# Two level products joined, small products moved, and a last norm by token blocks in a two-layer hybrid decoder kernel

## What is computed

```python
for l in range(2):
    h = rmsnorm(x, norm1)
    qa, ka, va, hb, gate_b, gate_c, qc, fc, ic, og, zg = split_in(h @ w_in)   # 1024 -> 6400 columns
    ya = dilated window attention of (rope(qa), rope(ka), va)                 # 3 groups, 2 heads of 64 each
    yb = gate_b * conv(gate_c * hb)
    log_f, kgate = forget gate of fc
    # gated linear recurrence, per head and chunk:
    #   att[t, s] = sum_c q[t, c] * k[s, c] * exp(b[t, c] - b[s, c])   for s <= t,  b = cumsum(log_f)
    oc, s_fin = hgrn2(qc, log_f, kgate, ic)
    mix = g0 * (ya @ w_pa) + g1 * (yb @ w_pb) + g2 * (yc @ w_pc)
    x = x + mix @ w_o
    x = x + square(relu(rmsnorm(x, norm2) @ w_up)) @ w_down
return rmsnorm(x, norm_f), new caches and states
```

## Time and profile before

| | us |
|---|---|
| median of 3 runs | 827.78 (827.65 to 829.39) |
| the profiled execution's own time | 829.25 |
| its span, first to last instruction | 827.5 |
| PE busy | 816.1 (99% of the span) |
| DVE busy | 570.0 (69%) |
| ACT busy | 436.8 (53%) |
| POOL busy | 264.2 (32%) |
| mean granted PE clock | 0.995 |

### The profile page before, as it was taken

One profiled execution on the slowest core, in us unless ns is written; L12 is line 12 of the kernel. 1 busy time (PEld: TensorE's weight loads), 2 busy tenths in 40 slices (PEclk: granted clock), 3 DMA queues, 4 the chain that ended last, 5 costly groups with the idle time before them and its releaser, 6 DMA issues.

```text
span 827.5 us, 18120 instructions
## 1 busy us (share of the span) xinstructions
PE 816.1 (99%) x7016; PEld 801.4 (97%) x7016; DVE 570.0 (69%) x768; ACT 436.8 (53%) x621; POOL 264.2 (32%) x230
## 2 busy tenths in 40 slices
PE   9999999999999999999999999999999999999995
PEld 8999999999999999999999999999999999999995
DVE  7778787676877666554576688957787776645553
ACT  6553376645557665434353634774555666643442
POOL 4585282036710000121147825801565000001220
PEclk9999999999999999999999999999999999999999
DMA  9896859767657778776659968887665876776751
GB/s 314 235 319 256 301 162 324 237 227 269 218 179 253 240 241 306 248 262 226 205 164 247 312 234 278 241 259 256 232 237 179 260 247 221 260 280 234 250 203 52
DMA packets 171035, 200.00 MB, mean 242 GB/s; under 512 B 19680, under 2 KB 168496, under 8 KB 169648
## 3 DMA queue, kind: packets, MB, share of 16 engines
q1 hardware_dynamic: 169584, 197.02, 72.4%
q10 hardware_dynamic: 1392, 2.15, 0.7%
HBM read 191.25 MB, written 51.90 MB: 294 GB/s over the span
## 4 chain that ended last, share of the span: by engine, by line
PE 95%; DVE 3%; DMA 0%; ACT 0%; issue 0%; DVEq 0%; ACTq 0%
PE main L644 28%; PE main L645 28%; PE main L646 27%; PE small L694 2%; PE small L660 1%; PE small L646 1%; PE small L645 1%; PE small L644 1%; DVE w_lo L1189 1%; PE small L705 1%; DVE h_lo L1205 0%; DMA raw<-in_w_in 0%; PE small L798 0%; PE small L853 0%; PE small L722 0%; PE main L615 0%
## 5 line engine op out<-in xcount | busy, mean ns | idle before, releaser
L954 ACT ACTIVATE w_hi<-raw 128x1024 fp32r<-128x1024 f32 (+1 forms) x256 | 266.2, 1041 | 247.9 <-PE main L646 186.9
L1189 DVE TENSOR_TENSOR w_lo<-raw,w_hi 128x1024 fp32r<-128x1024 f32 (+1 forms) x256 | 337.3, 1318 | 64.6 <-ACT w_hi L954 60.6
L644 PE MATMUL main<-h_hi,w_hi 128*128 128x264 f32 x1264 | 365.6, 289 | 0.9 <-DVE w_lo L1189 0.8
L645 PE MATMUL main<-h_lo,w_hi 128*128 128x264 f32 x1264 | 358.8, 284 | 0.0
L646 PE MATMUL main<-h_hi,w_lo 128*128 128x264 f32 x1264 | 358.6, 284 | 0.0
L644 PEld LDWEIGHTS main<-h_hi,w_hi 128*128 128x128 f32 x1264 | 238.7, 189 | 5.9 <-DVE w_lo L1189 1.7
L645 PEld LDWEIGHTS main<-h_lo,w_hi 128*128 128x128 f32 x1264 | 239.0, 189 | 0.2
L646 PEld LDWEIGHTS main<-h_hi,w_lo 128*128 128x128 f32 x1264 | 237.6, 188 | 0.0
L644 PE MATMUL main<-a_hi,w_hi 128*128 128x264 f32 x512 | 145.3, 284 | 0.0
L645 PE MATMUL main<-a_lo,w_hi 128*128 128x264 f32 x512 | 145.0, 283 | 0.0
L646 PE MATMUL main<-a_hi,w_lo 128*128 128x264 f32 x512 | 145.0, 283 | 0.0
(11 more groups left out here) (222 smaller groups left out, 1030.0 us busy)
## 6 DMA issues: line engine op xcount, KB each, us to landing
raw<-in_w_in SPq DMA_DIRECT2D x48, 1024.0 KB, 5.8
raw<-in_w_up SPq DMA_DIRECT2D x32, 1024.0 KB, 5.3
raw<-in_w_down SPq DMA_DIRECT2D x32, 1024.0 KB, 5.2
out_kvs<-in_cache SPq DMA_DIRECT2D x48, 512.0 KB
out_kvs<-in_cache SPq DMA_DIRECT2D x32, 496.0 KB
raw<-in_w_o SPq DMA_DIRECT2D x8, 1024.0 KB, 5.3
raw<-in_w_br SPq DMA_DIRECT2D x8, 768.0 KB, 5.1
gates<-q_scratch SPq DMA_DIRECT2D x4, 768.0 KB, 7.2
```

Of the source, the lines that this page charges most:

```text
L644: pe.matmul(out[:, 0:TOK], wh, rh, start=start and k == 0, stop=False)
L645: pe.matmul(out[:, 0:TOK], wh, rl, start=False, stop=False)
L954: act.activation(w_hi[:, slot(l, u), 0:k, :], raw_of(u, k), ACT.Copy).then_inc(w_hi_ready, 1)
L1189: dve.tensor_tensor(w_lo[:, slot(l, u), 0:k, :], raw_of(u, k), w_hi[:, slot(l, u), 0:k, :].bitcast(F32), ALU.subtract).then_inc(w_lo_ready, 1)
```

## The change

It has six parts. (1) Levels 0 and 1 of the recurrence become one group, `first_levels`, behind unit 8: 8 products with 192 moving columns, the queries of the diagonal (copied by ACT into `q_first` behind output 5) beside the scaled odd queries of level 1, against the same keys. Their turns are 3 to 6, one for each pair of heads and half; level 2 keeps 7 and 8. DVE masks them all behind output 9 (`mask_first_levels`): four copies of 128 x 256 and four of 127 x 128. (2) "state" goes from unit 18 to 19, "sample kv T" from 20 to 21, "kv T 1" and "kv T 2" from 26 to 28, "attend" from 33 to 35, each ahead of the small product that was there. ACT's copies and DVE's copy move along. (3) In the last norm the squares become the stationary operand and one column of ones the moving one, so that tokens lie on partitions: three columns of sums. Root and reciprocal work on 128 x 3; three products of the broadcast reciprocal with the identity bring it back onto all partitions in PSUM. (4) In the head, `split_lo` of unit 6 goes ahead of `bounds`, that of unit 7 ahead of the forget gate. (5) Units 6 and 7 of layer 0 also take their low products last. (6) ACT issues the first weight piece ahead of the gains. POOL no longer makes scaled keys for level 1 (they are the keys themselves) and waits for products only from level 4 on.

```diff
 TURNS = (
     ["norm1"]
     + ["values T", "sample values T"]
-    + [f"level {i} {h}" for i in range(9) for h in range(2)]
+    + [f"first levels {hp} {h}" for hp in range(2) for h in range(2)]
+    + [f"level {i} {h}" for i in range(2, 9) for h in range(2)]
...
+            def first_levels(l):
+                pe.wait_ge(kg_ready, l + 1)
+                pe.wait_ge(q_first_ready, l + 1)
+                pe.wait_ge(level_ready, l * 8 + 1)
+                w = P + HALF
+                for hp in range(2):
+                    banks = [use_bank(pe, l, f"first levels {hp} {h}") for h in range(2)]
+                    for tb in range(2):
+                        for h in range(2):
+                            rows = slice(h * HD, (h + 1) * HD)
+                            mm = pe.matmul(banks[h][:, tb * w:tb * w + w], kg[rows, hp, tb * P:tb * P + P],
+                                           q_first[rows, hp, tb, :], start=True, stop=True)
+                            if tb == 1:
+                                done(mm, f"first levels {hp} {h}")
...
-                if 7 <= u < 16:
+                if u == 8:
+                    first_levels(l)
+                if 9 <= u < 16:
                     level(l, u - 7)
...
-                if u == 18:
+                if u == 19:
                     pe.wait_ge(k_tm_ready, l + 1)
                     bank = use_bank(pe, l, "state")
...
-                if u == 20:
+                if u == 21:
                     z_ready(pe, l, CT_V + 2)
...
-                for at, g in ((24, 0), (26, 1), (26, 2)):
+                for at, g in ((24, 0), (28, 1), (28, 2)):
...
-                if u == 33:
+                if u == 35:
                     pe.wait_ge(kv_tm_ready, l * NG + NG)
                     attend(l)
-                if u == 35:
                     pe.wait_ge(s_probs, l + 1)
...
-                    if l == 0 and u < 6:
+                    if l == 0 and u < 8:
                         pe.wait_ge(out_taken, u + 1)
                         unit_lo_last(u, main[u % 4]).then_inc(w_used, 1)
+                        between(l, n)
                         continue
...
+            token_blocks = (0, P, TOK - P)
             pe.wait_ge(sq_ready, DEPTH * 2 + 1)
-            bank = use_bank(pe, DEPTH, "norm1")
-            pe.matmul(bank[:, 0:TOK], ones, sq_sum[:, :], start=True, stop=False)
+            bank = use_bank(pe, DEPTH, TURNS[0])
+            for b, t in enumerate(token_blocks):
+                pe.matmul(bank[:, b:b + 1], sq_sum[:, t:t + P], ones[:, 0:1], start=b == 0, stop=False)
             pe.wait_ge(last_square, 1)
-            done(pe.matmul(bank[:, 0:TOK], ones, rstd[:, :], start=False, stop=True), "norm1")
+            for b, t in enumerate(token_blocks):
+                mm = pe.matmul(bank[:, b:b + 1], rstd[:, t:t + P], ones[:, 0:1], start=False, stop=b == 2)
+            done(mm, TURNS[0])
+            pe.wait_ge(lb_step, 8)
+            bank = use_bank(pe, DEPTH, TURNS[1])
+            for b, c, n in ((0, 0, P), (1, 0, P), (2, P - SAMPLES, SAMPLES)):
+                mm = pe.matmul(bank[:, b * P:b * P + n], tok_std[:, 1, b:b + 1].to_broadcast([P, P]),
+                               ident[:, c:c + n], start=True, stop=True)
+            done(mm, TURNS[1])
...
+                if u == 5:
+                    z_ready(act, l, CT_CQ + 1)
+                    act.activation(q_first[:, :, :, 0:P], z[:, CT_CQ:CT_CQ + 2, 0:PROMPT].rearrange(
+                        "p a (b c) -> p a b c", b=2), ACT.Copy).then_inc(q_first_ready, 1)
...
+            act.dma_start(piece_raw(0), piece_source(0)).then_inc(piece_landed[0], 16)
             act.dma_start(cur[:, C_G1:C_G1 + KT], io["gain0"]).then_inc(gain_in, 16)
-            for i in range(3):
+            for i in range(1, 3):
...
-            norm_std(DEPTH, 0)
+            bank = take(act, DEPTH, TURNS[0])
+            act.activation(tok_std[:, 0, :], bank[:, 0:3], ACT.Sqrt, bias=eps[:, 0:1],
+                           scale=1.0 / D_MODEL).then_inc(std_ready, 1)
...
+                def mask_first_levels():
+                    dve.wait_ge(levels_in, 16)
+                    dve.wait_ge(att_clear, l + 1)
...
+                    for hp, h, name in parts:
+                        take(dve, l, name)
+                        wait_ends(dve)
+                        dve.copy_predicated(att[:, h, hp * 2:hp * 2 + 2, :], own.bitcast(U32), source(name)[:, :, 0:P])                           .then_inc(masked, 1)
+                    dve.wait_ge(masked, l * 20 + 4)
+                    for i, (hp, h, name) in enumerate(parts):
+                        late = att[:, h, hp * 2:hp * 2 + 2, :].rearrange("p b (n s) -> p b n s", s=2)[0:P - 1, :, :, 1]
+                        wait_ends(dve)
+                        dve.copy_predicated(late, last.bitcast(U32), source(name)[0:P - 1, :, P:P + HALF]).then_inc(masked, 1)
+                        dve.wait_ge(masked, l * 20 + 5 + i)
+                        dve.sem_inc(bank_taken[TURN[name] % 4], 1)
...
                     if u == 3:
+                        split_lo(l, at + 3)
                         if l == 0:
                             bounds()
                             new_params()
-                        split_lo(l, at + 3)
+                            split_lo(l, at + 4)
...
-                    if 8 <= u < 16:
+                    if u == 9:
+                        mask_first_levels()
+                    if 10 <= u < 16:
                         mask_level(u - 8)
...
-                    if u == 34:
+                    if u == 36:
                         bank = take(dve, l, "attend")
...
-            dve.reciprocal(rstd[:, :], rstd[:, :]).then_inc(lb_step, 1)
-            dve.wait_ge(lb_step, 8)
+            dve.reciprocal(tok_std[:, 1, :], tok_std[:, 0, :]).then_inc(lb_step, 1)
+            bank = take(dve, DEPTH, TURNS[1])
             for k in range(0, KT, 2):
                 dve.wait_ge(x_scaled, k + 2)
                 dve.tensor_tensor(x[:, k:k + 2, :], (u_relu, a_full)[k // RING][:, k % RING:k % RING + 2, :],
-                                  rstd[:, :].unsqueeze(1).to_broadcast([P, 2, TOK]), ALU.mult).then_inc(y_out, 1)
+                                  bank[:, 0:TOK].unsqueeze(1).to_broadcast([P, 2, TOK]), ALU.mult).then_inc(y_out, 1)
...
-                    if i >= 3:
+                    if i >= 4:
                         take(pool, l, f"level {i - 2} 1")
...
+                    if i == 1:
+                        def late(t):
+
+                            return t.rearrange("p h (b n s) -> p h b n s", b=2, s=2)[:, :, :, :, 1]
+                        step(pool.tensor_tensor(q_first[:, :, :, P:P + HALF], late(z[:, CT_CQ:CT_CQ + 2, 0:PROMPT]),
+                                                late(cum_f[:, :, :]), ALU.mult))
```

More of the change, by code:

```diff
@@ L687, in level @@
                         for h in range(2):
-                            kk, qq = operands(hp, h)
+                            rows = slice(h * HD, (h + 1) * HD)
+                            kk, qq = k_lv[rows, i % 2, hp, :], q_lv[rows, i % 2, hp, :]
                             if i == 8:
@@ L691, in level @@
                             else:
-                                c = (hp * 2 + tb) * w
-                                out, kk, qq = banks[h][0:early, c:c + w], kk[:, tb * P:tb * P + early], queries(qq, tb)
+                                c = (hp * 2 + tb) * HALF
+                                out, kk, qq = banks[h][0:early, c:c + HALF], kk[:, tb * P:tb * P + early], queries(qq, tb)
                             mm = pe.matmul(out, kk, qq, start=True, stop=True)
@@ L1038, in between @@
                         freed(f"sample kv T {i}", kv_s_ready, 2 * l + i + 1)
-                for at, g in ((25, 0), (27, 1), (27, 2)):
+                for at, g in ((25, 0), (29, 1), (29, 2)):
                     if u == at:
@@ L1265, in norm_inverse, with source @@
                     step(dve.reciprocal(rstd[:, :], rstd[:, :]))
+                def mask_first_levels():
+                    dve.wait_ge(levels_in, 16)
+                    dve.wait_ge(att_clear, l + 1)
+                    own = levels[:, 0:P].unsqueeze(1).to_broadcast([P, 2, P])
+                    last = levels[0:P - 1, P:P + HALF].unsqueeze(1).to_broadcast([P - 1, 2, HALF])
+                    parts = [(hp, h, f"first levels {hp} {h}") for hp in range(2) for h in range(2)]
+                    def source(name):
+                        return small[TURN[name] % 4][:, 0:2 * (P + HALF)].rearrange("p (b c) -> p b c", b=2)
+                    for hp, h, name in parts:
[9 more added lines that the diff above has]
+                        dve.sem_inc(bank_taken[TURN[name] % 4], 1)
                 def mask_level(i):
-                    if i == 0:
-                        dve.wait_ge(levels_in, 16)
-                        dve.wait_ge(att_clear, l + 1)
                     for h in range(2):
@@ L1275, in mask_level @@
```

(8 more changed lines are left out.)

50 lines of the change are left out of this document (15 added, 35 removed).

## The result

| | before | after |
|---|---|---|
| median | 828.56 us (4 runs) | 838.39 us (4 runs, 835.31 to 839.62) |
| profiled execution | 829.25 us | 839.62 us |
| its span | 827.5 us | 837.8 us |
| mean granted clock | 0.995 | 0.985 |

The ratio is 1.0114, 95% interval 1.0099 to 1.0129: the change makes the kernel 1.1% slower. Sign and mechanism are as forecast; the time is above the range of 829.0 to 836.0. The median of before is 828.56 here and not 827.78, because its four executions lie two and two in groups at 827.7 and 829.4.

The account below looks back on a forecast made before the run. PE, busy 99% of the span, was taken as the bound. Gains of -4.9 (head -1.5, joined products -1.7, moves -0.5, norm -1.2), waiting +7.0 and clock +3.2 gave +5.3 on 827.78: 833.1 us, range 829.0 to 836.0.

Parts of the forecast that it names:

- The wait at unit 9: PE stands still before level 2 until DVE's masks free two banks: 3.5 us a layer, +7.0 for both (5.2 to 8.2).
- The clock behind it: After the stop at unit 9 the clock falls once in each layer, 1.60 us a fall: +3.2 us (0 to 5).
- Rival (c): Clock comes back late as level 2's narrow products count little: 2.5 us a fall, 835 to 836; within two falls' 0.62.
- Head: Start of the kernel up to unit 7, parts 4 to 6: -1.5 us (-1.1 to -1.7).
- The 1.35 for the order: Head: units 6 and 7 of layer 0 no longer wait, so unit 7 ends 1.35 us earlier.
- the 0.15 for the transfer: Head: first weight piece issued ahead of the gains, ACT's 0.20 us wait for it shrinks; 0.15 us gained.
- The joined products: PE's own work on levels 0 and 1, 2.52 to 1.68 us: -0.84 a layer, -1.7 for both (-2.5 to -0.8).
- The moves: Moved groups save a changeover only at attend and sample probs T, -0.2 a layer; -0.5 us in all (0 to -0.9).
- The last norm: End of the kernel: 3.03 us removed, 1.74 added by the token-block norm; -1.2 us taken (-0.7 to -1.6).
- (a): Rival: clock stays up behind unit 9; 829.9 us with no fall (chance 0.12), 831.5 with one (0.16).
- (b): Rival: no wait or a short one at unit 9, gains stand alone, 822.9 us; chance 0.10.
- (d): Rival: 192 columns cost what 256 do and moves give nothing; gains 3.5, time 834.5 us; within two falls' 0.62.

Follow-up runs that it names:

- the first experiment: Changed kernel with the masks of the joined levels moved from behind unit 9 to behind unit 8, nothing else: 825.85 us, ratio 0.9961 to before.
- both mends: Changed kernel with masks of the joined levels behind unit 8 and the gains transfer issued ahead of the first weight piece: 824.09 us, ratio 0.9944 to before.

## Why the prediction was wrong

**The wait at unit 9** was read right. Forecast 3.5 us a layer, measured 3.28 and 3.27. The copies in DVE's timeline of after are the ones of the sum:

```profile
41.70 0.43 DVE L1249 TENSOR_TENSOR z<-main,rstd 128x264 f32<-128x264 f32 x1 [2.93 <-PE main L652]
42.05 1.42 DVE L1310 COPY_PREDICATED att<-levels,small 128x256 f32<-128x256 uint32 x4
43.62 0.44 DVE L1315 COPY_PREDICATED att<-levels,small 127x128 f32<-127x128 uint32 x1
44.30 0.44 DVE L1315 COPY_PREDICATED att<-levels,small 127x128 f32<-127x128 uint32 x1 [0.24 <-DVE att L1315]
```

0.35 from evacuation to copy, 1.42 for four copies (3 x 0.33 + 0.43), 0.44 for each late one, 0.24 between them: each within 0.02 of its term. Only the first late copy starts 0.15 behind the last own one where 0.26 had been taken, and the signal to PE came in 0.2. That one mask standing behind an evacuation that itself waits for PE turns into a stop of PE was the right step, and the first experiment shows that it carries the loss.

**The clock behind it** is the term that was mis-sized: 1.6 us a layer forecast, 3.1 in the profile of after, 3.0 us too little for both. The step that failed took the price of another event, the fall after 2 us of one-column products, for a fall after a full stop. That fall lasts about 3.5 us; the kernel after was at 1.2 GHz for twice as long in both layers, from inside the stop through level 2 and nearly all of unit 10, and paid twice as much. The lone run of the joined levels shows that the short fall does occur behind the stop too. Rival (c) had the effect (a clock that comes back late, 2.5 a fall) and the range was closed at its value, with no execution behind it that would have bounded a fall from above. Its reason, level 2's narrow products, isn't borne out: the lone run has the same products behind the same stop, and its clock came back in half the time. The sentence of the Trainium skill, "TensorE: Matmul & The Clock Gate", section "Why this matters for your kernels", that pauses between bursts be avoided, agrees with the traces: behind the stops of 3.3 us the clock fell in both layers of all three kernels profiled with them, though behind those of 2.63 us it didn't in either. The section "What's actually happening" of that page adds that what the gate goes by runs free of the kernel, so that the same work meets it at different points. The spread of the table above (2.9 to 6.8 us for one kernel) is in line with that; no run here shows the cause.

**The fall at unit 24** was left out: +1.6. Layer 1 had kept its clock in the one execution profiled, and the sum took that for a property of the kernel. The 21 executions of before on one chip show two groups of spans 1.5 apart, and the kernel with both mends has none in its profile and, to judge by the spans, one or more in two of its other executions. On that chip it is a matter of the execution; on the chip of the first experiment all nine executions of before have the longer time, so the chip or the session may have a part in it. Here is also a slip in the sum: the span of 827.5 that it was made against holds one such fall, and the median of 827.78 is the time of executions without it (825.9 + 1.75 = 827.65). Added to its own execution the sum gives 829.25 + 5.3 = 834.6; put onto a median without a fall it gave 833.1.

**Head**, forecast -1.5, measured -0.3. The 1.35 for the order is right: units 6 and 7 don't wait, and that edit alone brought unit 8 forward by 1.3. The step that failed is the 0.15 for the transfer. It looked at what the first piece could gain by coming earlier, and not at what the gains, moved to second place, hold up: ACT's first `h_hi`, the head of the chain. The cost was 0.8 to 1.0 us in the head (unit 8 at 33.91 against 33.07 with the gains first; values T at 33.50 against 32.50 between the two kernels with masks behind unit 8). The 1.5 in span holds 0.5 more that lies in the falls, for units 9 and 10 took 14.17 us in place of 14.66.

**The joined products** were right: -0.82 and -0.81 against -0.84. A group of sixteen took 1.50 in the chain, with 1.48 forecast. **The moves** were right where the saving was named: the stretch that holds `attend`, "sample probs T" and four units takes 14.43 us where it took 14.63. Of the -0.3 more in each layer, 0.26 is the one that comes with part 3, as its lone run shows, and nothing in the prediction foresaw it.

**The last norm**, forecast -1.2, was -0.8 in after's trace. The -1.2 of its own run holds 0.5 that lies far from the norm, as said there, and doesn't bear the forecast out. The chain of after, beside the earlier trace rows:

```profile
829.82 0.84 PE small L959 x6
...
830.68 0.27 ACT tok_std L1209
...
830.98 0.19 DVE tok_std L1600
...
831.21 0.85 PE small L964 x6
```

ACT and DVE are within 0.07 of their terms. The two groups on PE took 0.84 and 0.85, forecast 0.57 and 0.68 (0.8 with the signals on both sides). The six one-column products took 0.27 more than 0.052 each would have it, some 0.1 us for each instruction. The price by loaded columns of the Trainium skill, "TensorE: Matmul & The Clock Gate", section "LDWEIGHTS (loading the stationary operand)", agrees with this row; by it this part came to -0.5 in the prediction, so the measured -0.8 lies halfway between.

**The rivals.** (a), the clock stays up, holds for stops of a shorter kind (2.63 us, both layers of one execution) but not for the profiled execution of after. Of its other three the fastest (span 833.5) leaves 4.4 us for falls, too much for none; in how many layers they were isn't shown. (b) fell: the wait is there. (d) fell: the joined products gave their 1.6. The sum of the mis-sized terms, 3.0 (clock behind the wait) + 1.6 (second fall at unit 24) + 1.2 (head) + 0.4 (last norm) less 0.45 (wait) and 0.5 (moves and what comes with part 3), is 5.3 us, and 833.1 + 5.3 = 838.4. That this is the median of after to a tenth is partly chance: the terms come from its longest execution, and the slip of 1.5 above goes the other way.

## What to carry to other kernels

When a join of two groups ties up more banks for longer, look for the first group behind it that wants one, and for what the engine that frees it stands behind. If that is an evacuation of the unit just issued, move the freeing step ahead by a unit: one line was worth 1.5% here, and turned a loss of 1.1% into a gain of 0.4%. Price a stop of PE at 1.6 to 1.8 times its length where the kernel otherwise never stops, with a wide range around it: on the mean of four to six executions, and at this one place, stops of 1.7, 2.6 and 3.3 us a layer brought 0.6 to 0.8 of their own length again in clock ((4.2 - 1.7) / 3.4, (4.9 - 1.7) / 5.25 and (7.0 - 1.7) / 6.55). Before a difference is put onto a median, see whether the profiled execution and the median have the same number of falls. And when a part run alone gives the forecast number, look in its trace whether the gain lies where it was forecast.

## What the runs showed of the hardware

- The same stop of 3.3 us was followed by 1.5 us of lost time in the profile of one kernel and by 3.1 in that of another, where the clock had fallen within the stop and stayed low twice as long; a stop of 1.70 brought the clock down in one layer of one execution, and stops of 2.63 did not in two.
- A plain product of 256 columns on 128 partitions is two instructions of 0.22 us each (7.07 us for 32), twice the 0.107 of the 256-column instructions on alternating halves of 64 partitions in the earlier trace rows. The 16 instructions of 192 columns on alternating halves of 64 partitions took 0.08 to 0.09 each with their group's side cost left out, half of what 192 columns would take at 0.22 us for 256, so the two halves do overlap.
- A transfer of 4 KB issued first on ACT's queue landed after 2.3 us; issued second, behind one of 256 KB, after 4.3.
- With a run of 64 one-column products halved and a unit between (1.10 us each in place of 2.03), the profiled execution had no fall of the clock, and the spans of five executions lay within 0.7 us, less than a fall costs.
